# Final normalisation of a transformer layer: in a stage of its own, or inside the loop over expert blocks

## The chip, the cores and the metric

The kernel runs on one core of one Trainium2 chip. The metric is the device time of one execution in microseconds (us).

## What is computed

One layer of a decoder with 2048 tokens (T) and 1024 channels (D), all in float32: a normalisation, a combined projection, two kinds of attention, an output projection with the residual, and then a mixture of 32 experts of which each token uses two. At the end every row is normalised once more. What matters here:

```python
def rms_norm(x, g):
    y = x * lax.rsqrt(jnp.mean(x * x, axis=-1, keepdims=True) + EPS)
    return y * g

x = x + jnp.concatenate([o_diff, o_swa], axis=-1) @ w_out
n2 = rms_norm(x, norm2_g)
# router: top-1 group of 4, then top-2 experts inside the group, two gates for each token
# each expert e, on the rows xs of its tokens:
#   y = (silu(xs @ w_gate[e]) * (xs @ w_up[e])) @ w_down[e]
out = jnp.zeros((T + 1, D)).at[slot_tok].add(ys * slot_gate[:, None])[:T]
x = x + out
return rms_norm(x, final_g)
```

A token's row is complete when both of its experts have added to it.

## The kernel before

The program is a chain of stages; each is a function with one instruction stream for each engine (TensorE `pe`, VectorE `dve`, ScalarE `act`, GpSimd `pool`, and SyncE `sp`, which issues plain DMAs), joined by semaphores. Between stages stands a barrier. A float32 product is made of three, with each operand split in a high and a low part (`split_product`, L56 to L58); ScalarE copies the high part of a piece of weights, VectorE subtracts to get the low part (`low`, L1767).

`output_projection` (L994) works on 16 tiles of 128 tokens. It writes the residual rows to `acc_d` and the normalised rows to `n2_d` in HBM, and routes: `choose` finds a token's two experts, `place` their places in the lists, and GpSimd's `scatter` writes for each token and each of its two experts a pair (token, gate) into `slots_d`. The table has 32 x 16 blocks of 128 places and is filled beforehand with `empty`, whose tokens are the padding rows 2048 to 2175.

`experts` (L1567) loops over the 32 experts and, in each, over its blocks of 128 tokens; here there are 47 blocks. Expert e's weights are replaced by those of expert e+1, in 12 pieces, while its last block runs (`replaced`): that is so in 31 blocks. For block b:

- TensorE: the product with `w_gate` into `g_ps`; that with `w_up` in two halves into `u_ps`; `turn_h(b, 0)` (transposes of the first half of `hid`), `turn_x(b + 1)` (those of the next block's `x`), `turn_h(b, 1)`; then the product with `w_down` into `y_ps`.
- ScalarE: `Silu` of `g_ps` into `hid` (L1743), copies of `hT` and `xT`, and at the end `y`, which is `y_ps` times the gate `own[:, 1]` (L1751); pieces of weights between them (`highs`).
- VectorE: `hid` times `u_ps` in two halves (`hidden(b, 0)`, `hidden(b, 1)`, L1785), the low parts of `hT` and `xT`, and the pieces of weights (`lows`): 0 to 2 ahead of the first `hid`, 3 between the two, 4 to 11 behind.
- GpSimd, whose turn b is one block behind in what it stores:

```python
def one_block(b, e, replaced, here, after):
    pool.wait_ge(x_in, b * 16 + 16)
    gather(b + 1, within(after))            # rows of n2_d for the next block
    add(b)                                  # scatter y of block b-1, accumulating into acc_d
    pool.wait_ge(own_free, b * 16 + 48)     # that scatter has landed
    pool.tensor_copy(own, slots[here])      # (token, gate) of block b; own_ready
```

`own` holds the rows' tokens and gates. It is copied in turn b (L1704) and read by ScalarE for block b's `y` and by GpSimd's scatter of it in turn b+1 (L1694). `gather` is L1683 (`fetch`) and L1687. What decides when something runs is the order in which each engine's program stands, and its semaphores; there is no scheduler.

`combine` (L1873) is the last stage: it loads `acc_d` in six batches, squares and sums each of the 16 tiles on ScalarE (L1927), adds EPS and raises to the power -0.5 on GpSimd (`var`, `rstd`, L1914 and L1916), multiplies on VectorE (L1935) and stores each tile.

## Time and profile before

| what | value |
|---|---|
| median of 3 runs | 2276.89 us (2276.48 to 2285.67) |
| the profiled execution, its own time | 2276.58 us |
| its span, first to last instruction | 2274.8 us |
| TensorE matmuls busy | 2053.0 us (90%) |
| VectorE busy | 1316.1 us (58%) |
| ScalarE busy | 1117.1 us (49%) |
| GpSimd busy | 516.5 us (23%) |
| granted TensorE clock, mean | 0.954 of 2.4 GHz |
| expert stage | about 1326 to 2229 us of the span |
| last stage | 2229 to 2274.8 us |

The rows below are of this one profiled execution. A row of instructions in time gives start and duration in us, the engine, the line of the program, the operation, the written tile, `<-`, the tiles read, and in brackets how long the engine had been idle before it and on what. DMA-issuing on GpSimd shows as DMA_INDIRECT; its duration is that of issuing, not of the transfer.

### The profile page before, as it was taken

How to read it: one execution, taken by the hardware profiler on the slowest of the kernel's cores; microseconds unless marked ns; L12 is line 12 of the kernel's file. 1: busy time of each engine (PE TensorE's matmuls, PEld its weight loads, DVE VectorE, ACT ScalarE, POOL GpSimd, SP SyncE). 2: the span in 40 equal slices, each digit the busy share in tenths (PEclk: the TensorE clock that was granted, in tenths of full speed). 3: DMA queues.
4: the chain of work that ended last, by engine and by line, in shares of the span. 5: the costliest groups of instructions: out<-in, count | busy, mean ns of one | idle time of the engine just before them, and what ended most of it. 6: DMA issues, size and time to landing. Idle time of an engine off the chain costs nothing. (4 is left out here: it accounts for less than half of the span.)

```text
span 2274.8 us, 39112 instructions
## 1 busy us (share of the span) xinstructions
PE 2053.0 (90%) x12599; PEld 1740.2 (77%) x12600; DVE 1316.1 (58%) x2425; ACT 1117.1 (49%) x2395; POOL 516.5 (23%) x624
## 2 busy tenths in 40 slices
PE   5999999969999992997999949999999999999990
PEld 4888888847777772996887738888888888888880
DVE  5333333338889881663555549756666648666533
ACT  4111111128888881663333338656656547666443
POOL 0211111114343444100132221111111111111114
PEclk9999999979999996998999969999999999999995
DMA  6333333252213207333553379978888979998828
GB/s 209 94 96 99 104 97 95 84 156 82 88 57 83 59 12 186 96 84 91 179 185 132 120 232 345 362 242 279 289 274 290 296 221 331 303 324 256 273 47 313
DMA packets 299717, 407.44 MB, mean 179 GB/s; under 512 B 17248, under 2 KB 211552, under 8 KB 299616
## 3 DMA queue, kind: packets, MB, share of 16 engines
q1 hardware_dynamic: 279952, 349.76, 46.3%
q0 software_dynamic: 16176, 55.09, 10.3%
q10 hardware_dynamic: 3504, 1.51, 0.3%
q8 instruction: 46, 0.75, 0.1%
q14 instruction: 39, 0.32, 0.0%
HBM read 314.01 MB, written 92.83 MB: 179 GB/s over the span
## 5 line engine op out<-in xcount | busy, mean ns | idle before, releaser
L56 PE MATMUL proj<-w_in_lo,n1T_hi 128*128 128x512 f32 (+1 forms) x640 | 245.8, 384 | 16.4 <-DVE w_in_lo L254 16.4
L57 PE MATMUL proj<-w_in_hi,n1T_lo 128*128 128x512 f32 (+1 forms) x640 | 240.2, 375 | 0.0
L58 PE MATMUL proj<-w_in_hi,n1T_hi 128*128 128x512 f32 (+1 forms) x640 | 239.8, 375 | 0.0
L527 ACT ACTIVATE prob<-score,nmax 128x512 f32<-128x512 f32 (+3 forms) x344 | 207.7, 612 | 37.5 <-DVE nmax L613 34.8
L56 PE MATMUL u_ps<-wu_lo,xT_hi 128*128 128x256 f32 x752 | 209.1, 278 | 0.0
L58 PE MATMUL u_ps<-wu_hi,xT_hi 128*128 128x256 f32 x752 | 209.0, 278 | 0.0
L57 PE MATMUL u_ps<-wu_hi,xT_lo 128*128 128x256 f32 x752 | 209.0, 278 | 0.0
L1767 DVE TENSOR_TENSOR wg_lo<-raw_pieces,wg_hi 128x1024 fp32r<-128x1024 f32 x124 | 148.7, 1220 | 88.8 <-ACT wg_hi L1738 85.8
L566 POOL TENSOR_SCALAR prob<-prob,scale,lam 128x512 f32<-128x512 f32 (+3 forms) x172 | 147.8, 871 | 230.0 <-DVE scale L629 214.0
L613 DVE TENSOR_REDUCE nmax<-score 128x2 f32<-128x1024 f32 (+3 forms) x172 | 171.2, 995 | 18.1 <-PE score L656 10.6
L674 PE MATMUL o_ps<-v_sb,aT 128*128 128x128 f32 x1088 | 154.0, 279 | 5.3 <-ACT o_diff L554 4.0
L56 PE MATMUL y_ps<-wd_lo,hT_hi 128*128 128x512 f32 x376 | 154.0, 410 | 5.0 <-DVE hT_lo L1778 4.3
L56 PEld LDWEIGHTS proj<-w_in_lo,n1T_hi 128*128 128x128 f32 x640 | 121.5, 190 | 40.2 <-DVE w_in_lo L254 10.6
L56 PE MATMUL g_ps<-wg_lo,xT_hi 128*128 128x512 f32 x376 | 149.8, 398 | 2.4 <-DVE xT_lo L1772 2.4
L57 PE MATMUL g_ps<-wg_hi,xT_lo 128*128 128x512 f32 x376 | 149.5, 398 | 0.0
L58 PE MATMUL g_ps<-wg_hi,xT_hi 128*128 128x512 f32 x376 | 149.4, 397 | 0.0
L57 PE MATMUL y_ps<-wd_hi,hT_lo 128*128 128x512 f32 x376 | 149.0, 396 | 0.0
L58 PE MATMUL y_ps<-wd_hi,hT_hi 128*128 128x512 f32 x376 | 148.9, 396 | 0.0
L1767 DVE TENSOR_TENSOR wd_lo<-raw_pieces,wd_hi 128x1024 fp32r<-128x1024 f32 x128 | 147.9, 1216 | 0.0
L1694 POOL DMA_INDIRECT acc_scratch<-y,own x48 | 85.0, 1771 | 274.7 <-issue 263.4
L674 PEld LDWEIGHTS o_ps<-v_sb,aT 128*128 128x128 f32 x1088 | 137.3, 194 | 11.1 <-ACT o_diff L554 10.6
L57 PEld LDWEIGHTS u_ps<-wu_hi,xT_lo 128*128 128x128 f32 x752 | 142.2, 189 | 2.1
(232 smaller groups left out, 4956.4 us busy)
## 6 DMA issues: line engine op xcount, KB each, us to landing
raw_pieces<-in_w_down SPq DMA_DIRECT2D x64, 1024.0 KB
raw_pieces<-in_w_gate SPq DMA_DIRECT2D x62, 1024.0 KB
raw_pieces<-in_w_up SPq DMA_DIRECT2D x62, 1024.0 KB, 7.4
qk_scratch<-qkT SPq DMA_DIRECT2D x96, 256.0 KB, 2.3
x_sb<-in_x SPq DMA_DIRECT2D x16, 512.0 KB, 4.2
h<-in_x SPq DMA_DIRECT2D x16, 512.0 KB
acc_scratch<-h SPq DMA_DIRECT2D x16, 512.0 KB, 3.1
n_scratch<-n SPq DMA_DIRECT2D x16, 512.0 KB
```

Of the source, the lines that this page charges most:

```text
L56: pe.matmul(out, hi, w_lo, start=first, stop=False)
L57: pe.matmul(out, lo, w_hi, start=False, stop=False)
L58: return pe.matmul(out, hi, w_hi, start=False, stop=last)
L527: act.activation(prob[:, n % RING, c, 0:w], score[:, n % BUFS, c, 0:w], ACT.Exp, bias=nmax[:, c, n:n + 1], accum_out=part[:, c, n:n + 1]). ...
L566: pool.tensor_scalar(prob[:, u % RING, 1, 0:w], prob[:, u % RING, 1, 0:w], scale[:, 1, u:u + 1], lam[:, 5:6], ALU.mult, ALU.mult).then_inc ...
L613: dve.tensor_reduce(nmax[:, :, n:n + 1], score[:, n % BUFS, :, 0:w], AX.X, ALU.max, negate=True).then_inc(max_ready, 1)
L674: mm = pe.matmul(o_ps[:, :], aT[:, u % 2, b * P:(b + 1) * P], v[:, h, j // P + b, :], start=(u == FIRST[m] and b == 0), stop=(u == LAST[m] ...
L1694: pool.indirect_dma_start(acc_d, bass.IndirectOffsetOnAxis(ap=own[:, 0:1].bitcast(I32), axis=0), y[:, :], None, compute_op=ALU.add).then_i ...
L1767: dve.tensor_tensor(piece(LO, k), raw_piece(raw, k), piece(HI, k), ALU.subtract)\
```

## The change

The normalisation moves into `experts`, and `combine` goes. `place` gives each of a token's two pairs a third number: the token itself if this expert is the later of its two, and the token + 2048 otherwise, which is outside `acc_d`'s and `out`'s checked bounds. `slots`, `own` and `slots_d` become three wide; in `empty` the third number is a padding row.

In turn b GpSimd now does more. Once the scatter `add(b)` has landed, `move_on(b)` moves the indices on (`final_at` takes `whole_at`, `whole_at` takes `own[:, 2]`) before `own` is copied. Then comes `scale(b)` (`var`, `rstd`) for the rows gathered the turn before, then `fetch_whole(b)`, which gathers from `acc_d` the rows that block b-1 completed, and `store(b)`, which scatters the rows just normalised to `out`; rows with an index out of bounds are skipped in both. ScalarE squares and sums the gathered rows behind its `Silu`. VectorE's `normalize(b)` stands behind `hidden(b, 0)`. Behind the loop two more rounds empty the pipeline.

```diff
-        pair = sb("pair5", [P, TILES, TOPK, 2])
+        later = sb("later5", [P, TOPK])
+        pair = sb("pair5", [P, TILES, TOPK, 3])
...
+                    for k, op in ((0, ALU.is_lt), (1, ALU.is_gt)):
+                        dve.tensor_tensor(later[:, k:k + 1], eidx_f[:, s, 0:1], eidx_f[:, s, 1:2], op)\
+                            .then_inc(place_step, 1)
...
+                    dve.scalar_tensor_tensor(out=pair[:, t, :, 2].bitcast(I32), in0=later[:, :], scalar=float(SEQ),
+                                             in1=consts[:, 2, t:t + 1].to_broadcast([P, TOPK]),
+                                             op0=ALU.mult, op1=ALU.add).then_inc(place_step, 1)
...
-        slots = sb("slots6", [P, LISTED, 2])
+        slots = sb("slots6", [P, LISTED, 3])
...
+                sp.dma_start(g_bc[:, :], row_broadcast(final_g, D)).then_inc(g_in, 16)
...
+                def fetch_whole(b):
+                    pool.wait_ge(at_ready, b * 2 + 6)
+                    pool.wait_ge(final_ready, b + 2)
+                    pool.sem_inc(passed, 1)
+                    pool.indirect_dma_start(whole[:, :], None, acc_d,
+                                            bass.IndirectOffsetOnAxis(ap=whole_at[:, :], axis=0),
+                                            bounds_check=SEQ - 1, oob_is_err=False).then_inc(whole_in, 16)
+
+                def scale(b):
+                    pool.wait_ge(ss_ready, b + 1)
+                    pool.wait_ge(rstd_ready, b + 1)
+                    pool.tensor_tensor(var[:, :], ss[:, :], power[:, 1:2], ALU.add).then_inc(var_ready, 1)
+                    pool.wait_ge(var_ready, b + 1)
+                    pool.wait_ge(final_ready, b + 1)
+                    pool.tensor_tensor(rstd[:, :], var[:, :], power[:, 0:1], ALU.pow).then_inc(rstd_ready, 1)
+
+                def store(b):
+                    pool.wait_ge(at_ready, b * 2 + 6)
+                    pool.wait_ge(final_ready, b + 2)
+                    pool.sem_inc(passed, 1)
+                    pool.indirect_dma_start(out, bass.IndirectOffsetOnAxis(ap=final_at[:, :], axis=0),
+                                            final[:, :], None, bounds_check=SEQ - 1, oob_is_err=False)\
+                        .then_inc(stored, 16)
+
+                def move_on(b):
+                    pool.wait_ge(own_free, b * 16 + 48)
+                    pool.wait_ge(stored, b * 16 + 16)
+                    pool.wait_ge(whole_in, b * 16 + 16)
+                    pool.sem_inc(passed, 1)
+                    pool.tensor_copy(final_at[:, :], whole_at[:, :]).then_inc(at_ready, 1)
+                    pool.wait_ge(at_ready, b * 2 + 5)
+                    pool.sem_inc(passed, 1)
+                    pool.tensor_copy(whole_at[:, :], own[:, 2:3].bitcast(I32)).then_inc(at_ready, 1)
+                    pool.wait_ge(at_ready, b * 2 + 6)
+                    pool.sem_inc(passed, 1)
+
                 def one_block(b, e, replaced, here, after):
                     pool.wait_ge(x_in, b * 16 + 16)
                     pool.sem_inc(passed, 1)
                     gather(b + 1, within(after))
                     add(b)
-                    pool.wait_ge(own_free, b * 16 + 48)
-                    pool.sem_inc(passed, 1)
+                    move_on(b)
                     pool.tensor_copy(own[:, :].bitcast(I32), slots[:, bass.ds(within(here), 1), :].bitcast(I32))\
                         .then_inc(own_ready, 1)
+                    scale(b)
+                    fetch_whole(b)
+                    store(b)
...
+                pool.memset(whole[:, :], 0.0).then_inc(at_ready, 1)
+                pool.memset(final[:, :], 0.0).then_inc(at_ready, 1)
+                pool.tensor_copy(whole_at[:, :], own[:, 2:3].bitcast(I32)).then_inc(at_ready, 1)
+                pool.tensor_copy(final_at[:, :], own[:, 2:3].bitcast(I32)).then_inc(at_ready, 1)
+                pool.wait_ge(at_ready, 4)
+                pool.indirect_dma_start(whole[:, :], None, acc_d, bass.IndirectOffsetOnAxis(ap=whole_at[:, :], axis=0),
+                                        bounds_check=SEQ - 1, oob_is_err=False).then_inc(whole_in, 16)
+                pool.indirect_dma_start(out, bass.IndirectOffsetOnAxis(ap=final_at[:, :], axis=0), final[:, :], None,
+                                        bounds_check=SEQ - 1, oob_is_err=False).then_inc(stored, 16)
...
                 blocks = block_count(pool)
                 add(blocks)
-                pool.wait_ge(own_free, blocks * 16 + 48)
+                move_on(blocks)
+                scale(blocks)
+                fetch_whole(blocks)
+                store(blocks)
+                scale(blocks + 1)
+                pool.wait_ge(stored, blocks * 16 + 32)
+                pool.wait_ge(whole_in, blocks * 16 + 32)
+                pool.sem_inc(passed, 1)
+                pool.tensor_copy(final_at[:, :], whole_at[:, :]).then_inc(at_ready, 1)
+                pool.wait_ge(at_ready, blocks * 2 + 7)
+                pool.wait_ge(final_ready, blocks + 3)
+                pool.sem_inc(passed, 1)
+                pool.indirect_dma_start(out, bass.IndirectOffsetOnAxis(ap=final_at[:, :], axis=0), final[:, :], None,
+                                        bounds_check=SEQ - 1, oob_is_err=False).then_inc(stored, 16)
+                pool.wait_ge(stored, blocks * 16 + 48)
                 pool.wait_ge(x_in, blocks * 16 + 16)
 
+                def square(b):
+                    act.wait_ge(whole_in, b * 16 + 16)
+                    act.wait_ge(rstd_ready, b + 1)
+                    act.activation(sq[:, :], whole[:, :], ACT.Square, scale=1.0 / math.sqrt(D),
+                                   accum_out=ss[:, :]).then_inc(ss_ready, 1)
...
                     act.activation(hid[:, :], g_ps[:, :], ACT.Silu).then_inc(silu_ready, 1)
+                    square(b)
                     highs(3, 4, 5)
...
+                blocks = block_count(act)
+                square(blocks)
+                square(blocks + 1)
...
+                def normalize(b):
+                    dve.wait_ge(rstd_ready, b + 2)
+                    dve.wait_ge(stored, b * 16 + 16)
+                    dve.scalar_tensor_tensor(out=final[:, :], in0=whole[:, :], scalar=rstd[:, :], in1=g_bc[:, :],
+                                             op0=ALU.mult, op1=ALU.mult).then_inc(final_ready, 1)
...
                     hidden(b, 0)
+                    normalize(b)
                     lows(3)
...
+                blocks = block_count(dve)
+                normalize(blocks)
+                normalize(blocks + 1)
...
-def combine(nc, sem, acc_d, final_g, power, out):
...
-        combine(nc, sem, acc_d, final_g, power, out)
...
-    empty = np.zeros((P * LISTED, 2), np.float32)
-    empty[:, 0] = (SEQ + np.arange(P * LISTED) // LISTED).astype(np.int32).view(np.float32)
+    empty = np.zeros((P * LISTED, 3), np.float32)
+    empty[:, 2] = empty[:, 0] = (SEQ + np.arange(P * LISTED) // LISTED).astype(np.int32).view(np.float32)
```

On VectorE, in a block whose expert's weights are replaced, there stood before (`hid<-hid,u_ps` is `hidden`, first and second half; `lo` tiles are the split-off low parts):

```order
L1783 ISA [waits p6_silu_ready]
L1785 TENSOR_TENSOR hid<-hid,u_ps 128x256 [waits p6_u_done]
L1766 REGISTER_ALU
L1767 TENSOR_TENSOR wg_lo<-raw_pieces,wg_hi 128x1024 [waits w_hi_ready]
L1783 REGISTER_ALU
L1785 TENSOR_TENSOR hid<-hid,u_ps 128x256 [waits p6_u_done]
L1778 TENSOR_TENSOR hT_lo<-g_ps,hT_hi 128x256 [waits p6_hT_ready]
```

and now, in the same place:

```order
L1888 ISA [waits p6_silu_ready]
L1890 TENSOR_TENSOR hid<-hid,u_ps 128x256 [waits p6_u_done]
L1882 REGISTER_ALU
L1883 ISA [waits p6_rstd_ready]
L1884 SCALAR_TENSOR_TENSOR final<-whole,rstd,gf_bc 128x1024 [waits p6_stored]
L1865 REGISTER_ALU
L1866 TENSOR_TENSOR wg_lo<-raw_pieces,wg_hi 128x1024 [waits w_hi_ready]
L1888 REGISTER_ALU
L1890 TENSOR_TENSOR hid<-hid,u_ps 128x256 [waits p6_u_done]
L1877 TENSOR_TENSOR hT_lo<-g_ps,hT_hi 128x256 [waits p6_hT_ready]
```

The multiplication by `rstd` and the wait for it stand between the two halves of `hid`, ahead of `lows(3)`.

On GpSimd, a turn of the same kind was, from the copy of `fetch` on (`acc_scratch` is `acc_d`, `n_scratch` is `n2_d`):

```order
L1683 COPY fetch<-slots 128x1 [waits p6_x_in]
L1684 REGISTER_ALU
L1687 DMA x<-n_scratch,fetch 128x1024 [waits p6_x_turned,p6_fetch_ready]
L1691 REGISTER_ALU
L1694 DMA acc_scratch<-y,own 2176x1024 [waits p6_own_ready,p6_y_ready]
L1702 REGISTER_ALU
L1704 ISA [waits p6_own_free]
L1704 COPY own<-slots 128x2
```

and is now, from the scatter on:

```order
L1720 DMA acc_scratch<-y,own 2176x1024 [waits p6_own_ready,p6_y_ready]
L1748 REGISTER_ALU
L1752 COPY final_at<-whole_at 128x1 [waits p6_whole_in,p6_own_free,p6_stored]
L1753 ISA
L1755 COPY whole_at<-own 128x1 [waits p6_at_ready]
L1756 REGISTER_ALU
L1765 ISA [waits p6_at_ready]
L1765 COPY own<-slots 128x3
L1734 TENSOR_TENSOR var<-ss,power 128x1 [waits p6_rstd_ready,p6_ss_ready]
L1737 TENSOR_TENSOR rstd<-var,power 128x1 [waits p6_final_ready,p6_var_ready]
L1727 DMA whole<-acc_scratch,whole_at 128x1024 [waits p6_at_ready,p6_final_ready]
L1743 DMA out<-final,final_at 2048x1024 [waits p6_at_ready,p6_final_ready]
```

Two copies stand ahead of the copy of `own`, and two small operations and two indirect transfers behind it; the transfers wait for VectorE's `final`.

## Rows read from the trace of the kernel before

**Rows 1.** Windows: us, each engine's busy us (instructions), granted clock, DMA share, GB/s.

```profile
1439.00:1440.00 1.00, 1.00 (x4) 0.81 (x3) 1.00 (x2) 1.00 (x2) 0.44 (x1) 0.50 1.06 422
1700.00:1900.00 200.00, 199.83 (x1183) 173.38 (x1182) 126.76 (x139) 117.13 (x138) 35.62 (x44) 1.00 0.86 275
```

**Rows 2.** Timeline of GpSimd (POOL), 1720 to 1753 us.

```profile
1721.84 1.59 POOL L1694 DMA_INDIRECT acc_scratch<-y,own  x1 [6.31 <-issue]
1728.38 0.19 POOL L1704 COPY own<-slots 128x2 int32 x1 [4.95 <-DMA acc_scratch<-y,own]
...
1740.09 1.80 POOL L1694 DMA_INDIRECT acc_scratch<-y,own  x1 [6.31 <-issue]
1749.45 0.19 POOL L1704 COPY own<-slots 128x2 int32 x1 [7.55 <-DMA acc_scratch<-y,own]
1751.61 0.18 POOL L1683 COPY fetch<-slots 128x1 int32 x1 [1.98 <-issue]
1752.59 0.99 POOL L1687 DMA_INDIRECT x<-n_scratch,fetch  x1 [0.80 <-POOL fetch L1683]
```

**Rows 3.** Timeline of VectorE (DVE), 1727 to 1750 us.

```profile
1728.18 0.42 DVE L1785 TENSOR_TENSOR hid<-hid,u_ps 128x256 f32<-128x256 f32 x1 [1.82 <-PE u_ps L58]
1728.52 1.22 DVE L1767 TENSOR_TENSOR wg_lo<-raw_pieces,wg_hi 128x1024 fp32r<-128x1024 f32 x1
1730.90 0.42 DVE L1785 TENSOR_TENSOR hid<-hid,u_ps 128x256 f32<-128x256 f32 x1 [1.16 <-PE u_ps L58]
...
1749.34 0.42 DVE L1785 TENSOR_TENSOR hid<-hid,u_ps 128x256 f32<-128x256 f32 x1 [0.64 <-PE u_ps L58]
```

**Rows 4.** Timeline of TensorE (PE), around 1731 us.

```profile
1731.79 0.38 PE L1822 MATMUL u_ps<-ident,hid 128*128 128x128 f32 x2
```

**Rows 5.** GpSimd's groups by line in the expert stage: busy us, mean ns | idle before.

```profile
L1694 POOL DMA_INDIRECT acc_scratch<-y,own x48 | 85.0, 1771 | 274.7 <-issue 263.4 <-ACT y L1751 11.3
L1687 POOL DMA_INDIRECT x<-n_scratch,fetch x47 | 49.9, 1062 | 68.4 <-PE xT_ps L1814 49.7 <-POOL fetch L1683 15.8 <-issue 3.0
L1704 POOL COPY own<-slots 128x2 int32 x47 | 12.1, 258 | 315.3 <-DMA acc_scratch<-y,own 315.3
```

**Rows 6.** The scatter L1694 by itself: from issue to landing.

```profile
DMA to landing us min/median/max: 6.0/9.0/10.1
```

**Rows 7.** Groups by line, last stage; the last row is from the output projection.

```profile
L1935 DVE SCALAR_TENSOR_TENSOR o<-acc,rstd,gf_bc 128x1024 f32<-128x1024 f32 x16 | 20.6, 1284 | 33.4 <-DMA gf_bc<-in_final_g 22.5 <-POOL rstd L1916 10.9
L1916 POOL TENSOR_TENSOR rstd<-var,power 128x1 f32<-128x1 f32 x16 | 18.1, 1134 | 1.3
L1927 ACT ACTIVATE sq<-acc 128x1024 bf16<-128x1024 f32 x16 | 16.7, 1046 | 24.2 <-DMA acc<-acc_scratch 24.2
...
L1440 POOL TENSOR_TENSOR rstd<-var,power 128x1 f32<-128x1 f32 x16 | 9.1, 570 | 1.2
```

**Rows 8.** Timeline of TensorE around two of its waits, at 49 and at 1438 us.

```profile
49.67 0.50 PE L56 MATMUL proj<-w_in_lo,n1T_hi 128*128 128x512 f32 x1 [2.65 <-DVE w_in_lo L254]
...
1438.25 0.79 PE L56 MATMUL y_ps<-wd_lo,hT_hi 128*128 128x512 f32 x1 [2.96 <-DVE hT_lo L1778]
...
1441.70 0.39 PE L58 MATMUL y_ps<-wd_hi,hT_hi 128*128 128x512 f32 x1
...
1444.26 0.39 PE L57 MATMUL y_ps<-wd_hi,hT_lo 128*128 128x512 f32 x1
```

**Rows 9.** Who waited for whom in the expert stage: us, times, longest us.

```profile
ACT hT_hi L1729 <- PE g_ps L1822: 136.2, 45, 5.2
...
PE y_ps L56 <- DVE hT_lo L1778: 4.3, 2, 3.0
```

**Rows 10.** Timeline of GpSimd: the last scatter.

```profile
2218.06 1.58 POOL L1694 DMA_INDIRECT acc_scratch<-y,own  x1 [11.30 <-ACT y L1751]
```

**Rows 11.** DMA issues: KB each, median us from issue to landing.

```profile
acc<-acc_scratch SPq DMA_DIRECT2D x2, 512.0 KB, 4.9
...
slots<-slots_scratch POOLq DMA_DIRECT2D x1, 512.0 KB, 7.6
```

More of the change, by code:

```diff
@@ L1122, in output_projection @@
         CHOOSE = 12
-        PLACE = 9
+        PLACE = 12
         PLACED = TILES * PLACE
@@ L1278, in place @@
                                              op0=ALU.add, op1=ALU.mult).then_inc(place_step, 1)
-                    dve.wait_ge(place_step, base + 7)
+                    dve.wait_ge(place_step, base + 10)
                     dve.reciprocal(pair[:, t, 0, 1:2], den[:, :]).then_inc(place_step, 1)
-                    dve.wait_ge(place_step, base + 8)
+                    dve.wait_ge(place_step, base + 11)
                     dve.tensor_tensor(pair[:, t, 1, 1:2], pair[:, t, 0, 1:2], vexp[:, s:s + 1], ALU.mult)\
@@ L1564, in raw_piece, with experts @@
     return raw[:, k, :].rearrange("p (a b) -> p a b", a=(2, 4, 1)[k // 4])
-def experts(nc, sem, n2_d, acc_d, slots_d, empty_d, w_gate, w_up, w_down, ident, passed, wg, wu, starts, ends, hi_ready,
+def experts(nc, sem, n2_d, acc_d, slots_d, empty_d, final_g, power, out, w_gate, w_up, w_down, ident, passed, wg, wu, starts, ends, hi_ready,
             lo_ready):
@@ L1587, in experts @@
         wd = [sb(f"wd_{part}", [P, KF, D], F32R) for part in ("hi", "lo")]
-        slots = sb("slots6", [P, LISTED, 2])
+        slots = sb("slots6", [P, LISTED, 3])
         fetch = sb("fetch6", [P, 1], I32)
-        own = sb("own6", [P, 2])
+        own = sb("own6", [P, 3])
+        g_bc = sb("gf_bc", [P, D])
+        whole = sb("whole6", [P, D])
+        sq = sb("sq6", [P, D], BF16)
+        ss = sb("ss6", [P, 1])
+        var = sb("var6", [P, 1])
+        rstd = sb("rstd6", [P, 1])
+        final = sb("final6", [P, D])
+        whole_at = sb("whole_at6", [P, 1], I32)
+        final_at = sb("final_at6", [P, 1], I32)
         x = sb("x6", [P, D])
@@ L1622, in experts @@
         own_free = sem("p6_own_free")
+        g_in = sem("p6_g_in")
+        at_ready = sem("p6_at_ready")
+        whole_in = sem("p6_whole_in")
+        ss_ready = sem("p6_ss_ready")
+        var_ready = sem("p6_var_ready")
+        rstd_ready = sem("p6_rstd_ready")
+        final_ready = sem("p6_final_ready")
+        stored = sem("p6_stored")
         def block_count(eng):
@@ L1760, in _ @@
                 act.activation(warm[:, :], xT_hi[:, 0, 0:1].bitcast(F32), ACT.Silu)
+                act.sem_inc(rstd_ready, 1)
+                act.sem_inc(final_ready, 1)
                 over_experts(act, one_block)
+                blocks = block_count(act)
+                square(blocks)
+                square(blocks + 1)
             @block.vector
@@ L1806, in _ @@
                     low(0, k)
+                dve.wait_ge(g_in, 16)
                 over_experts(dve, one_block)
+                blocks = block_count(dve)
+                normalize(blocks)
+                normalize(blocks + 1)
             @block.tensor
@@ L1947, in build @@
     acc_d = nc.dram_tensor("acc_scratch", [SEQ + P, D], F32).ap()
-    slots_d = nc.dram_tensor("slots_scratch", [P * LISTED, 2], F32).ap()
+    slots_d = nc.dram_tensor("slots_scratch", [P * LISTED, 3], F32).ap()
     with ExitStack() as ctx:
@@ L1983, in build @@
                                   acc_d, slots_d, starts, ends, (w_gate, w_up, w_down), wg, wu, hi_ready, lo_ready)
-            experts(nc, sem, n2_d, acc_d, slots_d, empty, w_gate, w_up, w_down, ident_sb, passed, wg, wu, starts, ends,
+            experts(nc, sem, n2_d, acc_d, slots_d, empty, final_g, power, out, w_gate, w_up, w_down, ident_sb, passed, wg, wu, starts, ends,
                     hi_ready, lo_ready)
-        combine(nc, sem, acc_d, final_g, power, out)
 def constants():
```

62 lines of the change are left out of this document (3 added, 59 removed).

## The prediction

> **What bounds the kernel now.** I read the windows first. From 1700 to 1900 us, inside the expert stage, TensorE is busy 199.83 of 200 us at a granted clock of 1.00 (2.4 GHz), VectorE 127, ScalarE 117, GpSimd 36 [rows 1]. So TensorE bounds the expert stage, and any new wait on its path is paid in full; everything else there is cover. One block takes 18.25 us: that is the distance of the two accumulating scatters, 1721.84 and 1740.09 [rows 2]. The dropped last stage runs behind it with TensorE idle: from the last scatter, issued at 2218.06 [rows 10], to the end of the span at 2274.8 are 56.7 us.
>
> Next I read GpSimd's and VectorE's instructions in time [rows 2, 3]. In each block GpSimd issues the scatter of the last block's rows (`add`), waits until it has landed, and only then copies the new `own`. VectorE's second product `hid` (the second half) starts 9.06 us after the scatter's start (1730.90 against 1721.84). The `own` copy starts 6.5 us after it in one block and 9.4 us in the next (1749.45 against 1740.09), there even after that block's second `hid` at 1749.34. The landings of all 48 scatters lie between 6.0 and 10.1 us, with a median of 9.0 [rows 6]; 30 of the 47 blocks are of the long kind, those that follow a block that replaced weights, and 17 of the short. The mean comes from the grouped rows: 315.3 us of idle before 47 copies is 6.71 each, and the scatter itself is busy 1.77, so 8.48 us from scatter start to copy [rows 5]. Today nobody waits for that copy but ScalarE at the end of the block, so it costs nothing.
>
> **The change, part by part.** (1) *The new wait in the block.* `normalize(b)` stands on VectorE between the two `hid` products, and waits for `rstd` of `scale(b)`, which GpSimd runs behind `move_on(b)`, which waits for `add(b)` to land. So landing, copies, power, normalisation and second `hid` are now one chain. From where the `own` copy starts today: two added copies with their hand-over, 2 x 0.27 (a copy is 0.19 [rows 2]; 0.08 for a hand-over on the engine is my estimate, as the engine shows it between dependent instructions); the `own` copy 0.27; `var` 0.27; the power 0.57 [rows 7]; two hand-overs across engines 0.15; the normalisation 1.28 [rows 7]. Sum 3.1 us. In a block that replaces weights `lows(3)` also stands ahead of the second `hid`, 1.17 us more (1.22 busy, pipelined) [rows 3]. The second `hid` can start at 8.48 + 3.1 = 11.6 us after the scatter's start, or 12.75 with `lows(3)`. Its deadline: it starts at 9.06 now and ends at 1731.32, TensorE takes its transposes at 1731.79 because the transposes of `x` stand ahead [rows 4]; with 0.1 for the hand-over 0.35 us is spare, so 9.4. That makes it late by 2.2 us in the 16 blocks that replace nothing and 3.35 us in the 31 that do, and TensorE with it, because behind that `hid` come the transposes, the `y` product and the next block, in order on TensorE: 35 + 104 = 139, less 3 for the first block, whose scatter is issued before the stage is under way: **+136 us**. Queued behind the same wait on VectorE are the splits of `hT`, `xT` and eight pieces of weights; they keep their distance to the next block, since that moves with them.
>
> (2) *The clock.* At 1438.25 the trace has just such a stall by accident: TensorE waits 2.96 us between the transposes and the `y` product [rows 8], and the granted clock is then 0.50 (1.2 GHz) [rows 1]. The 8 matmuls from 1438.25 to 1441.70 take 3.45 us, where the next 11 take 2.56, 0.233 each: 1.6 us lost. A wait of 2.65 us (49.67) is followed by a first matmul of 0.50, not 0.79, and no such stretch. The 30 long blocks will wait 3.1 or 4.3 us (9.4 + 3.1 - 9.4, and 1.17 more), the short ones 0.3 or 1.5. I take a fall in 21 of the 30: **+33 us**; ends 0 and 48. The Trainium skill (TensorE: Matmul & The Clock Gate, HAM oscillation) describes a loop whose wait in each pass makes every next pass start at the lower clock; by that rule all 30 would pay, 48 us (rival B). The rows agree in the one case they have.
> I keep to 21 because the waits lie close above one that cost nothing.
>
> (3) *What the new work costs by itself.* ScalarE's square, 1.05 [rows 7] plus a short read-out, stands behind the activation; before its next step that TensorE needs, the copy of `hT`, ScalarE now waits 136.2 us in 45 blocks, 3.0 each [rows 9]: nothing. The square waits for the gathered `whole` of the block before, issued some 8 us before that block ends and 14 before the square; a plain load of that size lands in 4.9 us [rows 11]. GpSimd gets two indirect transfers a block. From the scatter's start in a long block: normalisation over at 12.4; two issues of 1.06 (the mean of the gather of `x` [rows 5]) with 0.8 ahead of each (1751.79 to 1752.59 [rows 2]), 16.1; the next expert's registers 1.97 (1749.64 to 1751.61) and `fetch` 0.18, 18.3; the gather of `x`, 20.1; ready for the next scatter at 20.9, against a block of 21.4 to 22.6 us. Covered, by only 0.5 to 2 us. Traffic: 8 MB are read and 8 MB written either way. TensorE sees none of it while DMA keeps its present level (0.86 busy). Two waits of TensorE for `hT_lo`, 4.3 us [rows 9], come where weights are late, and with the clock's 1.6 they make 5.9; longer blocks leave time for the weights: **-5 us**.
>
> (4) *The start.* `slots` grows from 512 to 768 KB. It lands in 7.6 us [rows 11] ahead of the first gather, when TensorE idles; half as much again is at most 3.8. Three tiny VectorE steps for each tile hide behind the projection except in the last, 0.3. **+2.5 us**.
>
> (5) *The end.* From the last scatter's start (2218.06): lands 6.5 later (the short kind [rows 2]), copies, `var`, power 1.4, normalisation 1.3, then gather 0.8 + 5.5 (4.9 for a plain load, 7.6 for the other [rows 11]), square 1.3, `var` and power 0.9, normalisation 1.3, scatter 0.8 + 6: 25.8 us, so 2244 where it is 2274.8: **-31 us**, ends -27 and -34. Once only: the barriers, sixteen powers and loads of the old stage go.
>
> Sum on the profiled execution: span 2274.8 + 136 + 33 - 5 + 2.5 - 31 = 2410; its own time is 1.8 above its span: **2412 us**. The median of the runs, 2276.89, is 0.3 above that execution's 2276.58, which is nothing here.
>
> *Bounds of what the trace doesn't show.* The chain of 3.1 could be 2.75 (copies that pipeline) or 3.75: in the last stage, with VectorE at work beside it, the power takes 1.13 on average, 0.57 in the output projection [rows 7]; I take 0.57, since VectorE waits at that moment. That is -17 to +30 us. The Trainium skill (GPSIMD Engine Reference, Specifications) says that GpSimd contends with VectorE instructions that have two SBUF inputs; the difference of 0.57 and 1.13 agrees. By it the copies in short blocks, where VectorE still splits weights, would be slow too.
>
> **The rivals.** *A, faster: the wait is hidden.* VectorE stands idle before both `hid` products; if `rstd` is there early enough, the normalisation fits between them and the end's 31 us are kept: 2276.6 - 31 + 2.5 = 2248. It decides at an `own` copy 9.4 - 3.1 = 6.3 us after the scatter's start (5.1 with `lows(3)`). For it: the shortest landing is 6.0 [rows 6], and blocks of the short kind that replace nothing are nearly free. Against it: the mean is 8.48 [rows 5], and nothing in the change makes a scatter land earlier.
>
> *B, the clock falls in all 30 long blocks.* 48 us for 33: 2427. For it: all their waits are longer than the one of 2.96. *The clock never falls*: 2379. For it: the wait of 2.65 us that cost nothing; against it, 1438.25.
>
> *C, GpSimd becomes the bound.* If an indirect transfer with a bounds check takes 2.5 us to issue, not 1.06, GpSimd's turn ends 2.9 us later, some 1.5 beyond its slack, and each of 47 blocks grows by that much, 70 us: 2482. For it: the accumulating scatter takes 1.77 for as many rows [rows 5]. Against: with 1.77 it still about fits.
>
> *D, landings shorten.* If longer blocks leave the DMA queues emptier, the long landing goes from 9.4 toward 6.5; half of that in 30 blocks takes back 43 us and most of the clock's part: 2345.
>
> **How the numbers follow.** Forecast 0.42 (its own range 2390 to 2440), B 0.20 for the fall in all and 0.11 for none, C 0.10, D 0.12, A 0.04, and 0.01 that gains and losses cancel. The range reaches from the low bound without a fall of the clock (2412 - 33 - 17 = 2362) to the high bound with all of it (2412 + 30 + 15 = 2457) and a quarter of C's 70 (2475); outside lie A, most of C and part of D. About 0.5% is what a measurement of this kernel can tell from no change. Faster by over 0.5% is A: 0.04. Within it: 0.01. Slower: 0.95.
>
> **What would show it.** Right: VectorE's waits list the normalisation on GpSimd's `rstd` with 2 to 4 us in nearly each block; TensorE waits for `hid` or `hT_lo` some 110 to 140 us in all; the granted clock drops in the expert stage; scatters lie 19.5 to 24 us apart; from the last scatter's start to the end it is near 26 us. Wrong: TensorE still over 99% busy in the experts; GpSimd's scatter starting more than 2.5 us after `y` is ready (that is C); or a landing under 6 us.

## The result, and the profile after

The changed kernel takes **2484.23 us** (median of 4 runs, 2479.41 to 2493.73) beside 2278.8 us for the kernel before (4 runs on the same chip, 2276.48 to 2285.67): a ratio of 1.089, 95% interval 1.0865 to 1.0915. The forecast was 2412 us, range 2362 to 2475. The direction and the place are right; the time lies above the range. The profiled execution of the changed kernel took 2493.73 us, 9.5 more than its median, with a span of 2491.9.

The waits of the changed kernel (engine, line, tile, what it waited for: us in all, times, longest):

```profile
POOL final_at L1752 <- DMA acc_scratch<-y,own: 345.0, 48, 9.3
...
DVE final L1884 <- POOL rstd L1737: 234.7, 48, 13.3
...
PE u_ps L1932 <- DVE hid L1890: 172.8, 44, 9.7
...
POOL whole L1727 <- DVE final L1884: 110.6, 48, 2.3
```

GpSimd waits for the landing, VectorE for GpSimd's `rstd`, TensorE for VectorE's second `hid`. It is the chain that the prediction laid out, and only its last link costs time. Before, TensorE had no wait for `hid`; its waits for `hT_lo`, 4.3 us [rows 9], are gone here.

Windows over the stretch from the first scatter to the last, before and then after (columns as in [rows 1]):

```profile
1346.50:2218.00 871.50, 864.23 (x5076) 748.98 (x5076) 566.72 (x612) 523.39 (x612) 153.34 (x186) 0.99 0.85 276
```

```profile
1357.00:2467.00 1110.00, 932.72 (x5076) 794.63 (x5076) 620.01 (x659) 574.30 (x708) 328.90 (x469) 0.92 0.73 231
1700.00:1900.00 200.00, 164.82 (x923) 141.21 (x921) 106.03 (x114) 101.51 (x126) 58.62 (x85) 0.91 0.74 234
```

Both have the same 5076 matmuls. With the exact times of the first and last scatter, the stretch grew from 871.57 to 1109.47 us, by 237.9. TensorE stood idle for 176.8 us of it where it was 7.3 (+169.4), and was busy 932.7 where it was 864.2 (+68.5) with the same work, that is, at a lower clock: 0.92 for 0.99. This split into **waits** and **clock** is used for every run below. The rest of the 217.1 us between the two spans: the first scatter starts 10.5 us later (1357.03 for 1346.49), and from the last scatter to the end it is 25.4 us where it was 56.7 (-31.3). 169.4 + 68.5 + 10.5 - 31.3 = 217.1.

One long block. GpSimd's timeline of the changed kernel, 1910 to 1937 us:

```profile
1912.06 3.30 POOL L1720 DMA_INDIRECT acc_scratch<-y,own  x1 [6.59 <-issue]
1923.48 0.18 POOL L1752 COPY final_at<-whole_at 128x1 int32<-128x1 int32 x1 [8.12 <-DMA acc_scratch<-y,own]
1923.84 0.18 POOL L1755 COPY whole_at<-own 128x1 int32<-128x1 int32 x1 [0.17 <-POOL final_at L1752]
1924.31 0.19 POOL L1765 COPY own<-slots 128x3 int32 x1 [0.29 <-POOL whole_at L1755]
1924.45 0.18 POOL L1734 TENSOR_TENSOR var<-ss,power 128x1 f32<-128x1 f32 x1
1924.72 0.57 POOL L1737 TENSOR_TENSOR rstd<-var,power 128x1 f32<-128x1 f32 x1
1927.61 1.10 POOL L1727 DMA_INDIRECT whole<-acc_scratch,whole_at  x1 [2.32 <-DVE final L1884]
...
1936.84 1.59 POOL L1720 DMA_INDIRECT acc_scratch<-y,own  x1 [4.81 <-issue]
```

VectorE's timeline of the same block:

```profile
1918.48 0.42 DVE L1890 TENSOR_TENSOR hid<-hid,u_ps 128x256 f32<-128x256 f32 x1 [4.58 <-PE u_ps L58]
1925.42 1.28 DVE L1884 SCALAR_TENSOR_TENSOR final<-whole,rstd,gf_bc 128x1024 f32<-128x1024 f32 x1 [6.52 <-POOL rstd L1737]
1926.63 0.42 DVE L1890 TENSOR_TENSOR hid<-hid,u_ps 128x256 f32<-128x256 f32 x1
```

And TensorE's:

```profile
1921.33 1.04 PE L1924 MATMUL xT_ps<-ident,x 128*128 128x128 f32 x8
1927.10 0.68 PE L1932 MATMUL u_ps<-ident,hid 128*128 128x128 f32 x2 [4.74 <-DVE hid L1890]
1927.62 0.79 PE L56 MATMUL y_ps<-wd_lo,hT_hi 128*128 128x512 f32 x1
1928.20 0.63 PE L57 MATMUL y_ps<-wd_hi,hT_lo 128*128 128x512 f32 x1
...
1930.68 0.39 PE L57 MATMUL y_ps<-wd_hi,hT_lo 128*128 128x512 f32 x1
```

Read the three together. The scatter starts at 1912.06 and is seen as landed at 1923.48, 11.4 us later, where the longest landing of [rows 6] was 10.1 and [rows 2] had 9.4 from start to copy. From there to the second `hid` at 1926.63 are 3.15 us. TensorE has stood for 4.74 us, and its next matmuls take 0.63 instead of 0.39. The granted clock says so, in a window of 1 us there and one behind it (clock: third number from the end):

```profile
1928.60:1929.60 1.00, 1.00 (x4) 0.78 (x3) 0.51 (x2) 0.50 (x1) 0.70 (x2) 0.50 0.06 1
1931.00:1932.00 1.00, 1.00 (x6) 0.82 (x5) 0.00 (x0) 0.00 (x0) 0.97 (x1) 1.00 0.84 340
```

The lower level (1.2 GHz) is granted behind the wait and the higher one (2.4 GHz) again by 1931. It falls so in 30 of 47 blocks (counted as blocks whose `y` product has more than two steps over 0.35 us from matmul to matmul); before it was 1. They are the 30 blocks of the long kind: TensorE's wait just ahead is 3.2 to 9.7 us in them, 5.3 on average, and at most 1.3 us in the other 17.

The end, on GpSimd, answers to [rows 10]:

```profile
2466.50 1.58 POOL L1720 DMA_INDIRECT acc_scratch<-y,own  x1 [5.30 <-issue]
2472.84 0.18 POOL L1752 COPY final_at<-whole_at 128x1 int32<-128x1 int32 x1 [4.75 <-DMA acc_scratch<-y,own]
...
2476.77 1.09 POOL L1727 DMA_INDIRECT whole<-acc_scratch,whole_at  x1 [2.32 <-DVE final L1884]
...
2484.59 1.04 POOL L1802 DMA_INDIRECT out<-final,final_at  x1 [2.18 <-DVE final L1884]
```

### The profile page after: what moved, and what is told of

The parts are those of the page before. It is cut to its first block and busy times, and to the rows that moved or that the text cites. A ratio compares the mean times of both kernels' runs of the same rounds, so it can differ in the third digit from the quotient of the medians.

```text
span 2491.9 us, 40183 instructions
## 1 busy us (share of the span) xinstructions
PE 2125.9 (85%) x12599; PEld 1789.5 (72%) x12600; DVE 1356.3 (54%) x2506; ACT 1150.7 (46%) x2461; POOL 676.8 (27%) x890
## 5 line engine op out<-in xcount | busy, mean ns | idle before, releaser
L1884 DVE SCALAR_TENSOR_TENSOR final<-whole,rstd,gf_bc 128x1024 f32<-128x1024 f32 x49 | 62.9, 1285 | 234.7 <-POOL rstd L1737 234.7
L613 DVE TENSOR_REDUCE nmax<-score 128x2 f32<-128x1024 f32 (+3 forms) x172 | 171.3, 996 | 17.6 <-PE score L656 10.1
L56 PE MATMUL y_ps<-wd_lo,hT_hi 128*128 128x512 f32 x376 | 178.6, 475 | 1.6
L1720 POOL DMA_INDIRECT acc_scratch<-y,own x48 | 109.4, 2280 | 250.9 <-issue 246.4
L1932 PE MATMUL u_ps<-ident,hid 128*128 128x128 f32 x94 | 26.8, 378 | 172.8 <-DVE hid L1890 172.8
L57 PE MATMUL y_ps<-wd_hi,hT_lo 128*128 128x512 f32 x376 | 169.9, 452 | 0.0
L58 PE MATMUL y_ps<-wd_hi,hT_hi 128*128 128x512 f32 x376 | 167.9, 446 | 0.0
L56 PEld LDWEIGHTS proj<-w_in_lo,n1T_hi 128*128 128x128 f32 x640 | 122.6, 192 | 40.5 <-DVE w_in_lo L254 11.1
```

The source lines that it names most:

```text
L56: pe.matmul(out, hi, w_lo, start=first, stop=False)
L57: pe.matmul(out, lo, w_hi, start=False, stop=False)
L58: return pe.matmul(out, hi, w_hi, start=False, stop=last)
L613: dve.tensor_reduce(nmax[:, :, n:n + 1], score[:, n % BUFS, :, 0:w], AX.X, ALU.max, negate=True).then_inc(max_ready, 1)
L1720: pool.indirect_dma_start(acc_d, bass.IndirectOffsetOnAxis(ap=own[:, 0:1].bitcast(I32), axis=0), y[:, :], None, compute_op=ALU.add).then_i ...
L1884: dve.scalar_tensor_tensor(out=final[:, :], in0=whole[:, :], scalar=rstd[:, :], in1=g_bc[:, :], op0=ALU.mult, op1=ALU.mult).then_inc(final ...
```

## The experiments

Two questions. Is the wait of VectorE for `rstd`, which stands behind the landing, what costs, or is it the added work? And why are the waits and the clock's part larger than forecast? In the table, "stretch" is first scatter to last in the profiled execution, "idle" and "busy" are TensorE's in it, "falls" the blocks in which the clock fell, and "long" the mean from scatter start to the copy behind its landing in the long kind of block (over 8 us, number of blocks in brackets, the first block left out). Each split is that of one profiled execution. Of the first row, the time is the median beside the changed kernel; the ratios are each to the kernel before on the same chip, taken beside it.

| kernel | time, us | ratio to before, 95% | stretch | idle | busy | falls | long |
|---|---|---|---|---|---|---|---|
| before | 2278.8 | 1 | 871.6 | 7.3 | 864.2 | 1 | 9.53 (30) |
| changed | 2484.2 | 1.0865 to 1.0915 | 1109.5 | 176.8 | 932.7 | 30 | 11.27 (30) |
| `rstd` ahead of the landing | 2269.2 | 0.9924 to 0.9962 | 889.3 | 18.3 | 871.0 | 1 | 9.90 (30) |
| normalisation late | 2333.6 | 1.0208 to 1.0252 | 955.2 | 67.0 | 888.2 | 9 | 10.46 (40) |
| both moves | 2300.4 | 1.0074 to 1.0118 | 906.5 | 35.0 | 871.5 | 2 | 10.31 (40) |
| filled wait | 2453.9 | 1.0726 to 1.0788 | 1071.8 | 62.4 | 1009.3 | 12 | 10.38 (30) |
| no rows moved | 2473.1 | 1.0813 to 1.0869 | 1091.3 | 163.2 | 928.2 | 29 | 10.78 (30) |
| `w_down` held back | 2412.6 | 1.0551 to 1.0593 | 1037.3 | 123.3 | 914.0 | 25 | 9.46 (29) |
| `w_up` and `w_down` held back | 2375.4 | 1.038 to 1.0473 | 991.6 | 89.6 | 902.1 | 16 | none |

**`rstd` ahead of the landing.** In the changed kernel GpSimd runs `scale` ahead of `move_on`; the needed sum of squares is there long before, since `whole` was gathered a block earlier.

```diff
                     add(b)
+                    scale(b)
                     move_on(b)
...
-                    scale(b)
                     fetch_whole(b)
```

> Theory M (the cost is VectorE's wait for rstd, which GpSimd computes only behind the landing of the accumulating scatter): scale(b) needs only ScalarE's square, which ends some 7.6 us into the block, so rstd is ready about 8.7 us in, when the first hid ends; only the normalisation's 1.3 us and lows(3) stay ahead of the second hid. VectorE's wait for rstd falls from 228 us to under 40, TensorE's wait for hid from 173 us to under 30, no fall of the clock; time 2250 to 2285. Rival W (the added work between the two hid products costs, not the wait: 1.3 us on VectorE in 47 blocks, two more transfers on GpSimd): time stays over 2400. Rival T (the 16 MB of rows that now move inside the expert stage crowd out weights and scatters): time stays over 2400, landings of the long kind still near 11.3 us.

Measured: 2269.24 us (9 runs), 0.9943 of the 2282.96 us that the kernel before took beside it: 0.6% faster than before, with an interval clear of 1, and within the expected 2250 to 2285. Its waits:

```profile
DVE final L1884 <- POOL rstd L1737: 28.4, 19, 13.2
...
POOL var L1734 <- ACT sq L1812: 176.9, 48, 8.7
...
POOL final_at L1752 <- DMA acc_scratch<-y,own: 99.5, 41, 7.5
...
PE u_ps L1932 <- DVE hid L1890: 7.4, 16, 1.3
```

This is the outcome of the theory that blames the wait, and speaks against the one that blames the work. VectorE's wait for `rstd` goes from 234.7 to 28.4 us, TensorE's for `hid` from 172.8 to 7.4, and GpSimd now waits for the square first and for the landing afterwards, with nobody behind it. All the work of the change is still there: both transfers, both small operations, the square, the normalisation. So the added work costs 889.3 - 871.6 = 17.7 us in the stretch, and the order on GpSimd the other 220. The timeline of GpSimd in this kernel has a price of its own:

```profile
1903.34 1.81 POOL L1720 DMA_INDIRECT acc_scratch<-y,own  x1 [4.95 <-issue]
1908.73 0.68 POOL L1734 TENSOR_TENSOR var<-ss,power 128x1 f32<-128x1 f32 x1 [3.58 <-ACT sq L1812]
1909.49 1.44 POOL L1737 TENSOR_TENSOR rstd<-var,power 128x1 f32<-128x1 f32 x1
1912.81 0.72 POOL L1752 COPY final_at<-whole_at 128x1 int32<-128x1 int32 x1 [1.88 <-DMA acc_scratch<-y,own]
```

The power takes 1.44 us and not 0.57, `var` 0.68 and not 0.18. VectorE now splits weights beside them instead of waiting: 7 of the 49 powers take 1.44 us, and these are just the ones beside which VectorE runs a subtraction `wg_lo<-raw_pieces,wg_hi`; the other 42 take 0.57 to 0.58.

**Normalisation late.** In the changed kernel VectorE normalises behind the split of the turned `x`, out of the way of `hid`; `rstd` still comes behind the landing.

```diff
                     hidden(b, 0)
-                    normalize(b)
...
                     split_xT(b + 1)
+                    normalize(b)
```

> Only VectorE's order differs: normalize(b) behind split_xT(b+1). Theory M: rstd still waits for the landing (11 us into the block plus 1.4), but that is earlier than split_xT ends (15 to 16 us into it), and no product of this block stands behind it any more. TensorE's wait for hid under 15 us, no fall of the clock, time 2245 to 2275. If GpSimd's turn, which now ends some 2 us later, becomes the bound, scatters start later than 2.2 us into the block and the time is 2280 to 2330. Rival W: VectorE does the same work, so TensorE would go on waiting for late weights, over 2350. Rival T: over 2400.

Measured: 2333.62 us (4 runs). The wait has moved to GpSimd and to the gather of `x` behind it:

```profile
PE xT_ps L1924 <- DMA x<-n_scratch,fetch: 66.5, 31, 24.0
...
PE g_ps L1932 <- DVE hid L1890: 18.7, 13, 2.5
...
POOL whole L1727 <- DVE final L1884: 124.7, 48, 8.9
```

24.0 of the 66.5 are the first block's, which every kernel has (24.3 in the changed one). GpSimd's turn has become the period: it idles 14.4 us ahead of its scatters, where the changed kernel has 246.4. So 150 of the 205 us can be had on VectorE alone, but not all. The expectation had 2245 to 2275 if only VectorE's wait counts, and 2280 to 2330 if GpSimd's turn becomes the bound; the second is the case, 4 us above its range. The clock fell in 9 blocks, where none was expected.

**Both moves.** The two edits above together.

> Edit: both moves together: GpSimd computes rstd before it waits for the landing, and VectorE normalises behind the split of the turned x. Nothing is left out. Theory M alone (what costs is a wait on VectorE ahead of the second hid): the 28 us that VectorE still waits for rstd with the first move vanish from TensorE's path, TensorE's wait for hid is under 3 us, and the time is 2255 to 2268 us. Rival G (GpSimd's turn is the second limit: its gather of whole and its store wait for the normalisation, the gather of x stands behind them, as in the run with the late normalisation alone, 2333.6 us): VectorE's normalisation comes some 6 us later than in the first move alone, TensorE waits for x in about 30 blocks, and the time is 2290 to 2335 us.

Measured: 2300.38 us (4 runs), 31 us slower than the first move alone. TensorE's wait for `x`, and GpSimd's for the normalisation:

```profile
PE xT_ps L1924 <- DMA x<-n_scratch,fetch: 54.1, 23, 23.7
...
POOL whole L1727 <- DVE final L1884: 61.4, 23, 7.2
```

With `rstd` early, the place between the two `hid` is the better one: a later normalisation only delays GpSimd's transfers. This is rival G's outcome, with TensorE waiting for `x` in 22 blocks beside the first instead of about 30. In both kernels with the late normalisation ten more blocks have a long landing (40 for 30); no run asks why.

**Filled wait.** 24 transposes of the identity into a spare PSUM tile ahead of the transposes of the second `hid`, to keep TensorE at work in the wait. They change no result.

```diff
+        spare_ps = ps("spare_ps", [P, 512])
...
                     turn_x(b + 1)
+                    for _ in range(24):
+                        pe.transpose(spare_ps[:, 0:P], ident[:, :], ident[:, :])
                     turn_h(b, 1)
```

> 24 more transposes of a constant tile into an unused PSUM tile (2.6 us at full clock) stand on TensorE in each of the 47 blocks where it waits for the second hid. If the waits are what makes the granted clock fall, then the 30 falls vanish or nearly so, the y products of all 47 blocks take 258 us and not 312, and although 2.6 us of work are added per block the time falls: minus 55 to 65 us for the clock, plus some 25 us in the 17 short blocks, whose wait is shorter than the filling: 2440 to 2460. If the clock follows something else: more than 10 falls stay and the time is above 2484.

Measured: 2453.9 us (2 runs). The time from the first to the last matmul of the `y` products, summed over 47 blocks, is 258.5 us before, 312.1 in the changed kernel (+53.6), and 274.4 here; falls go from 30 to 12. The time is in the expected range (2440 to 2460), but the falls don't vanish as expected, and more than 10 stay, which was half of the other theory's sign (the other half, a time above 2484 us, isn't met): the filling keeps the clock up in part of the blocks only. The sum shrinks by 37.7 us: 18 falls fewer give back 2.1 us each. By that price the 30 falls cost 63 us, beside the 68.5 of busy time. That the stretch, too, shrinks by 37.7 us is chance: the long landings are 0.9 us shorter in it as well, and the filling, 2.78 us, is longer than the wait of the short blocks.

**No rows moved.** The loop's gather of `whole` and its store keep their instructions, but a bound of 0 skips all rows except row 0, so that nearly all of `out` is not written. It asks if their traffic makes the landings longer.

```diff
-                                            bounds_check=SEQ - 1, oob_is_err=False).then_inc(whole_in, 16)
+                                            bounds_check=0, oob_is_err=False).then_inc(whole_in, 16)
```

The store has the same edit.

> As the change, but the bounds check of the two new transfers inside the loop lets only row 0 through: the gather of finished rows and the store of normalised rows move nearly no data, all instructions and waits stay (most rows of the output are not written). The long landings of the scatter grew from 9.5 to 11.3 us with the change. Theory Q (the scatter waits behind the rows that now move in the same queue, and in turn beside the weights): the long landings go back to 9.3 to 9.8 us, TensorE's waits fall by 30 x 1.7 = 50 us, time about 2425 to 2440. Rival (the landings grew because of the number of transfers issued, or of the new rhythm of the weights): landings stay over 11 us, time within 10 us of the change. Rival T: far less than 2425.

Measured: 2473.13 us (2 runs), 11 us less; long landings 10.78 us for 11.27, between the two expectations (9.3 to 9.8, and over 11) and nearer the second. The bytes of the two transfers are at most 0.5 of the 1.74 us by which the long kind grew, and not even that is clear: in the 14 blocks of each kernel in which the weight loads are issued at the same distance from the scatter (`w_up` 3.0 us ahead, `w_down` 1.5 behind), the mean is 10.75 us with the rows and 10.75 without, and two landings of 13.5 and 15.1 us among the others of the changed kernel make up part of the 0.5. Most is something else.

**`w_down` held back.** The next suspect was the weights' own traffic: the first of SyncE's two `w_down` loads is issued on average 0.50 us behind the start of a long scatter in the changed kernel, 1.34 before, the second some 2.4 us after it. Here SyncE issues them only when that scatter has landed.

```diff
+                    first = sp.value_load(starts[0:1, bass.ds(e, 1)], min_val=0, max_val=BLOCKS - 1)
                     for j in range(PAIRS):
                         sp.wait_ge(*lo_there(e, 2 * j + 1))
+                        if j == 4:
+                            sp.wait_ge(own_free, first * 16 + 48)
                         load(e + 1, j)
```

> Edit: in the changed kernel SyncE waits, before it issues an expert's two w_down loads for the next one, until the scatter that runs at that moment has landed. Nothing is left out. Theory L (the long landings are those that share the queues with the w_down loads, issued 0.5 us after the scatter's start): the 30 long landings fall from 11.27 us to the short kind's 6.4, the second hid is then at 6.4 + 3.14 or 4.37, late against 9.4 by at most 1.4 us; TensorE's wait for hid falls from 172.8 us to some 50, the clock falls in hardly any block, and the time is 2484 - 122 - 50 = about 2310 us, later by as much as the w_down weights now come late. Rival N (the length belongs to the scatter itself or to the w_up loads already under way): long landings stay within 0.7 us of 11.27, TensorE's wait stays above 140 us, and the time is 2470 to 2510 us.

Measured: 2412.62 us (5 runs), 72 us less than the changed kernel; long landings 9.46 us. It is between the two expectations: theory L had 6.4 and rival N over 10.5. Part of the length is `w_down`; the rest was left to `w_up`, already under way. The clock still fell in 25 blocks.

**`w_up` and `w_down` held back.** The same with `j == 2` in place of `j == 4`.

> Edit: as in the run that holds back the w_down loads until the scatter has landed (long landings 9.46 us there, 2412.6 us), but the two w_up loads, which are issued some 4.5 us ahead of the scatter, are held back too. Nothing is left out. Theory L2 (the rest of the long landing over the short one, 9.46 against 6.57, is the queue of w_up bytes still under way): all landings are of the short kind, 6.4 to 6.8 us; TensorE's wait for hid, 118 us there, falls below 60, the clock falls in under 10 blocks; the weights now come up to 12 us later and may cost: 2310 to 2370 us. Rival N2 (the rest belongs to the scatter itself, its rows or its additions): long landings stay at 9 us or more, and the time within 10 us of 2412.

Measured: 2375.39 us (4 runs). The DMA issue rows (line of the median: us from issue to landing), first of the changed kernel, then of this one:

```profile
raw_pieces<-in_w_up SPq DMA_DIRECT2D x62, 1024.0 KB, 7.6
...
acc_scratch<-y,own POOLq DMA_INDIRECT x48, 10.4
```

```profile
raw_pieces<-in_w_up SPq DMA_DIRECT2D x62, 1024.0 KB, 6.5
...
acc_scratch<-y,own POOLq DMA_INDIRECT x48, 6.3
```

All landings are now of the short kind, 6.49 us from start to copy, as theory L2 had it (6.4 to 6.8). The weights come late instead:

```profile
PE y_ps L56 <- DVE hT_lo L1880: 42.7, 16, 3.1
PE u_ps L1935 <- DVE hid L1893: 42.1, 34, 2.3
```

The wait for `hid` is 42.1 us where it was 172.8, as the expectation had it (under 60), and the time is 5 us above its 2310 to 2370: 16 blocks now wait for pieces of weights, and the clock falls in 16, where under 10 were expected.

**The table alone.** The kernel before with the third number in `pair`, `slots` and `own` and the three added steps of `place`, and nothing else.

```diff
-        slots = sb("slots6", [P, LISTED, 2])
+        slots = sb("slots6", [P, LISTED, 3])
...
-        PLACE = 9
+        PLACE = 12
```

> Edit: the kernel before with the third number in the table of slots, in pair and in own, and the three added steps of place, and nothing else of the change. Nothing is left out. By the prediction's term for the start, +2.5 us: 2281 us beside 2279, a ratio of 1.0011. Rival: the whole delay of the first scatter between the two profiled executions, 10.5 us, belongs to the table: a ratio of 1.0046. If it is spread between executions, the ratio is within 0.002 of 1.

Measured: 2282.47 us (12 runs) beside 2280.62 (17 runs), ratio 1.0012, interval 0.9999 to 1.0024. In its profiled execution the first scatter starts at 1348.17, 1.7 us later than before.

## Why the prediction was wrong, step by step

**The sign and the mechanism: right.** One chain from the landing over `rstd` and the normalisation to the second `hid`, with TensorE behind it. The first experiment shows it by itself: with `rstd` ahead of the landing, the same work takes 0.9943 of the time before, 13 us less on the same chip, instead of 205 us more.

**Term (1), the chain behind the landing: right.** Forecast 3.1 us from the first copy to the second `hid`, 4.27 with `lows(3)`; measured 3.14 and 4.37. The power ran in 0.57 us, as taken, because VectorE was waiting.

**Term (1), the landing itself: the step that failed.** The sum took the landings from the trace of before, 8.48 us from start to copy on average, as if the changed rhythm left them alone. They became 9.51: the short kind stayed (6.61 to 6.40), the long kind went from 9.53 to 11.27. 1.03 us in 47 blocks is 48 us, and +136 - 5 + 48 = 179 is set against 169.4 measured. The deadline of 9.4 us was a little too early: a second `hid` that starts 9.8 us behind the scatter would have cost TensorE no wait (in one long block it starts 10.61 + 4.37 = 14.98 us behind it, and TensorE waits 5.21). That takes off 0.4 us in 44 blocks. The prediction had only a rival in which landings shorten (D), and no upper bound for this term in its range. What makes a landing long is shown: the weight loads beside it. In the changed kernel it is 6.49 without them, 9.46 with `w_up` alone, 11.27 with both.

The kernel with `w_down` held back is nearly the case that the forecast described: long landings of 9.46 us, for the 9.4 taken, and a time of 2412.6 us, for 2412. That it is so near is in part chance. TensorE's idle time grew by 116 us in it, for the 131 of the forecast, its busy time by 49.8, for 33, its profiled execution took 10 us more than its median, and the loads that are held back are a change of their own.

**Why the long kind grew by 1.74 us** is for the most part open. The spacing of scatter and loads is some of it: in the changed kernel half of the long scatters meet their loads earlier than 3.0 us ahead and 1.5 behind, and land in 11.7 us on average, where the others take 10.75. With fewer falls of the clock (filled wait) the long kind is 0.9 shorter, and the first `w_down` load is issued 1.17 us behind the scatter's start instead of 0.50. But at one and the same spacing (`w_up` 3.0 us ahead, `w_down` 1.5 behind) the landing is 9.2 to 10.0 us before, mean 9.49 of 26, and 10.3 to 11.1 in the changed kernel, mean 10.75 of 14: 1.26 of the 1.74 us are not the spacing. The packets in the traces give a hint. In the 3 us ahead of such a scatter SyncE's queue moves 664 KB before (9.49 us), 558 with `rstd` first (9.80), 394 with the filled wait (10.25), 311 in the changed kernel (10.75) and 321 with no rows moved (10.75). The less of the loads is through when the scatter starts, the longer it takes. No run changes this by itself, so it is not shown to be the cause.

**Term (2), the clock: the mechanism right, the size half.** Forecast 33 us, 21 of 30 long blocks at 1.6; measured 68.5 of busy time, 30 of 30 at 2.1 to 2.3. Rival B had the count right (all 30) and a better price with it, 48 us. By the rule that it drew on (the Trainium skill, TensorE: Matmul & The Clock Gate, HAM oscillation) every pass behind such a wait starts slow, and the trace agrees: 30 of the 30 long blocks. The one wait of 2.65 us without a fall, on which the forecast leaned, had been in another stage, and the waits here came out longer than the forecast's 3.1 or 4.3: 159.5 us in the 30 long blocks, 5.3 each. The price was too low because the 1.6 counted eight matmuls of one accidental fall; here the two transposes ahead of them are slow too (0.68 us, where [rows 4] has 0.38), and so are the matmuls up to the clock's return.

**Term (3), new work hidden: right for GpSimd in this order.** It idles 246.4 us ahead of its scatters, so rival C did not happen; the gather of `whole` took 1.18 us and the store 1.02 to issue, for the 1.06 taken. The 5 us taken off for late weights are there, as far as a row shows them: the 4.3 us of [rows 9] went. The slack is thin all the same: move the normalisation back and C is what one gets (2333.6 and 2300.4).

**Term (4), the start: not contradicted.** Forecast +2.5 us; the table alone costs 1.0012, 2.7 us, though its interval reaches to nothing. The 10.5 us by which the first scatter is later in the profiled execution can't be put down to the change: 9.1 of them are there when TensorE ends the stage before (1328.6 for 1319.5), and the other kernels above with the same code up to that point end it anywhere from 1320.5 (the table alone) to 1330.9. Within the stage the load of `slots` takes 8.6 us for 7.6.

**Term (5), the end: right.** Forecast 25.8 us from the last scatter's start, -31; measured 25.4, -31.3.

**The sum.** Forecast 136 + 33 - 5 + 2.5 - 31 = 135.5 against 217.1 in the profiled executions: 38 from the waits (landings), 35 from the clock, 8 from the time ahead of the stage. Two terms missed upwards together, and they are linked: longer landings make longer waits, behind which the clock falls more often (all 30 at 11.27 us, 25 at 9.46), and with 18 falls fewer the landings were 0.9 us shorter. The range had bounds for the chain and for the clock, and none for the landing.

**Rival A** (2248 us, the wait hidden and the end's gain kept) did not happen, but the kernel with `rstd` first comes near it: 2269. What it misses is 18 us in the stretch, where VectorE still waits 28.4 us for `rstd` and a power beside its work takes up to 1.44 us.

## What to carry to other kernels

A small result that a tight engine needs must not be computed behind a wait for a transfer which it doesn't depend on: moving two tiny operations ahead of the landing was worth 215 us here, and moving their reader was worth less, because another queue then waited. When a change puts a DMA's completion on the critical path for the first time, its duration in the old trace is only a lower guide: look at what else is issued around it, and give it an upper bound, for the waiting itself shifts the spacing. Waits of 3 us and more that return in each pass (3.2 to 9.7 here) should be priced with the clock that they cost in all passes.

## What the runs showed of the hardware beyond that

- **An accumulating scatter of 128 rows of 4 KB** lands 6.5 us after its start with no weight load beside it, 9.5 with two loads of 1 MB issued ahead of it, and with two more issued behind its start 11.3 in the changed kernel, but 9.5 in the one before. The Trainium skill (DMA: Bandwidth & Descriptors, Queues, rings and completion order) says that a DMA engine takes turns, packet by packet, between the queues that have work; the trace agrees: the scatter was slowed and not held until the loads were through, since the last `w_down` load landed on average 13.6 us after its start and the scatter itself 11.1.
- **Issuing it** takes 1.6 to 1.8 us mostly, but in the changed kernel up to 7.4, with a mean of 2.28, and in 13 of 30 long blocks over 2.5: the block above has 3.30. With the weights held back the longest of 48 is 2.04. The kernel with the table alone also has one of 7.7.
- **Rows skipped by the bounds check** save nothing in issue: 1.22 us for the gather and 1.02 for the store, for 1.18 and 1.02 with the rows, and the time is only 11 us less.
- **Transposes of the identity kept the clock up in part of the blocks.** 24 of them in the wait (2.8 us) took away 18 of 30 falls. Shorter landings alone don't explain it: they are 10.38 us there, and with 9.46 (`w_down` held back) 25 falls stay. The Trainium skill (TensorE: Matmul & The Clock Gate, Part 4: PE-mode transpose) says that a transpose doesn't count as PE-busy the same way as a matmul; these, in fp32, had an effect on the clock all the same.
